# Expert tiles of 32 slots instead of 64: four column tiles, rows gathered for two experts at once, results scattered in 1 KB pieces

## The chip, the core and the metric

The kernel runs on one core of a Trainium2 chip. The time is that of one execution on the device in microseconds. Three runs of the kernel before took 806.93, 801.02 and 805.67 us; the median is 805.67.

## What is computed

One layer of a decoder for 256 prompt tokens and 8 sample tokens (T = 264) with 1024 features, all in fp32. The change touches the last part alone, the mixture of experts: each token chooses one of 4 groups and in it the best 2 of 8 experts, so 528 pairs of token and expert over 32 experts.

```
a = jnp.einsum('bld,edf->blef', h, w_gate)       # w_gate, w_up: 32 x 1024 x 256
u = jnp.einsum('bld,edf->blef', h, w_up)
act = jax.nn.silu(a) * u * combine[..., None]
return jnp.einsum('blef,efd->bld', act, w_down)  # w_down: 32 x 256 x 1024
```

Each expert's weights are 3 MB (1 MB each for gate, up and down). With the inputs of the reference an expert is chosen by 10 to 22 tokens, 16.5 in the mean; this follows from the reference's routing.

## The kernel before

Ahead of the experts stand the input projection, retention, block-sparse attention, output projections and the router. They read their weights through a ring of six 1 MB slots and end at about 510 us. Then VectorE works out the routing in a chain of small instructions and TensorE the positions of the tokens in each expert (L1093). A one-hot product, `row_table` (L1096 to L1101), writes for each expert and each of `CAP` = 64 slots the token that sits there. It is made twice, for output partitions 0 to 63 and 64 to 127. VectorE turns the first into `tidx_i` (L1505 to L1509, semaphore `t_idx`), the rows to gather, and the second into `sidx_i`, the rows to scatter to (L1510 to L1513). A slot without a token has an index out of bounds, and nothing is moved for it.

An expert then takes these steps. GpSimd gathers 64 rows of 4 KB into `xg` (L569 to L573). TensorE transposes them in eight pieces (`x_tr`, L1119) and VectorE copies them to `xgT` (`x_copy`). `gate_up` (L1129) holds the 64 rows as weights of a column tile of the array: two column tiles take the two halves of the 256 hidden columns of gate and up, 16 matmuls of 256 columns. An fp32 matmul is two instructions in the trace. ScalarE applies silu, VectorE multiplies (`hidden`), TensorE turns the result (`h_tr`, L1141), ScalarE copies it (`h_copy`), and `down` (L1147) makes the output in two column tiles, 4 matmuls of 512 columns. VectorE copies it out of PSUM (`y_copy`), and GpSimd scatters 128 pieces of 2 KB to `y_rows` (L574 to L577).

On TensorE the order for expert e is: gate and up of e, turned rows of e + 1, down of e - 1, turn of the hidden part of e (L1174 to L1179). Weights come through SyncE's queue into `SETS` = 5 sets of buffers; a set's gate and up are loaded again once `e_GU` says that they were used (L454 to L460), its down once `e_D` does. The first five sets are loaded during the stages before.

More tokens than slots would be served by overflow tiles: `XT = (2 * T) // (CAP + 1)` of them at most, 8. After expert 31 every engine goes through a loop of `XT` rounds (on SyncE and TensorE `XT // 2` rounds of two) and skips the bodies above the number of tiles that there are, none with these inputs (L596, L803, L1187, L1605). In the main stage VectorE also makes the tables for these tiles (`tile_counts`, `tile_tables`, `tile_experts`, `tile_rows`).

After the loop GpSimd waits for the scatters and signals `y_all` (L610 to L612). SyncE and ScalarE then read `y_rows` back, VectorE adds the two results of each token to the residual, and a last RMSNorm ends the kernel.

## Time and profile before

| | us |
|---|---|
| runs | 806.93, 801.02, 805.67 (median 805.67) |
| profiled execution, its time | 807.25 |
| its span, first to last instruction | 805.3 |
| TensorE matmuls busy | 694.6 (86%) |
| VectorE, ScalarE, GpSimd busy | 313.2, 129.4, 216.0 |
| mean granted TensorE clock | 0.947 |

HBM reads are 241.37 MB and writes 17.50 MB over the span. Busy TensorE counts matmuls whose ends are modelled and which overlap, so a high share does not say that it is the bound. The chain of work that ended last gives TensorE 49%, DMA 17%, VectorE 17%, the wait of SyncE's queue 7%, GpSimd 5%.

### The profile page before, as it was taken

How to read it: one execution, taken by the hardware profiler on the slowest of the kernel's cores; microseconds unless marked ns; L12 is line 12 of the kernel's file. 1: busy time of each engine (PE TensorE's matmuls, PEld its weight loads, DVE VectorE, ACT ScalarE, POOL GpSimd, SP SyncE). 2: the span in 40 equal slices, each digit the busy share in tenths (PEclk: the TensorE clock that was granted, in tenths of full speed). 3: DMA queues.
4: the chain of work that ended last, by engine and by line, in shares of the span. 5: the costliest groups of instructions: out<-in, count | busy, mean ns of one | idle time of the engine just before them, and what ended most of it. 6: DMA issues, size and time to landing. Idle time of an engine off the chain costs nothing.

```text
span 805.3 us, 11725 instructions
## 1 busy us (share of the span) xinstructions
PE 694.6 (86%) x3847; PEld 484.4 (60%) x3847; DVE 313.2 (39%) x1539; ACT 129.4 (16%) x381; POOL 216.0 (27%) x401
## 2 busy tenths in 40 slices
PE   3999996898999969999898999579999998888860
PEld 1888875687888756734434877355555554555530
DVE  2000895998768745600000221623432222112116
ACT  3122221232326222200010000300000000000001
POOL 0288992994000213200000000012222221221210
PEclk9999999899999989999999999769999999999995
DMA  9744899889977998579999794529999999999914
GB/s 314 197 147 139 287 332 386 300 290 332 340 270 246 340 373 278 176 292 406 400 409 364 232 420 189 210 85 382 394 398 395 398 381 388 402 398 399 357 70 161
DMA packets 98270, 247.21 MB, mean 307 GB/s; under 512 B 12156, under 2 KB 57852, under 8 KB 89890
## 3 DMA queue, kind: packets, MB, share of 16 engines
q1 hardware_dynamic: 83874, 220.28, 74.0%
q0 software_dynamic: 9456, 19.29, 7.2%
q10 hardware_dynamic: 4880, 6.88, 2.5%
q8 instruction: 32, 0.52, 0.3%
q14 instruction: 28, 0.23, 0.1%
HBM read 241.37 MB, written 17.50 MB: 321 GB/s over the span
## 4 chain that ended last, share of the span: by engine, by line
PE 49%; DMA 17%; DVE 17%; SPq 7%; POOL 5%; issue 3%; ACT 1%; POOLq 0%; DVEq 0%; ACTq 0%
PE zps L851 22%; DVE kall L1243 10%; PE nps L1136 10%; DMA ring_all<-in_w_up 6%; SPq L420 5%; DMA ring_all<-in_w_ret_o 4%; PE nps L1015 3%; PE zps L1126 2%; DMA kall<-in_cache_k 2%; PE bps L1156 2%; PE mps L1156 2%; DMA gain<-v_rows 2%; SPq L424 2%; PE zps L829 1%; DMA xs<-in_state_ret 1%
## 5 line engine op out<-in xcount | busy, mean ns | idle before, releaser
L851 PE MATMUL zps<-hT,ring_all 128*128 128x264 f32 x1152 | 279.1, 397 | 1.6 <-DVE hT L1424 1.0
L851 PEld LDWEIGHTS zps<-hT,ring_all 128*128 128x128 f32 x1152 | 220.6, 196 | 45.2 <-issue 3.7
L1243 DVE CUSTOM_DVE_ANT_0 kall<-kall,qb 128x128 f32<-128x128 f32 x512 | 141.1, 342 | 84.9 <-DMA kall<-in_cache_k 82.1
L570 POOL DMA_INDIRECT zatt<-h_rows,tidx_i x32 | 30.6, 956 | 217.6 <-DVEq L1509 200.1
L575 POOL DMA_INDIRECT y_rows<-zatt,sidx_i x32 | 32.5, 1015 | 172.4 <-DVE zatt L1582 172.4
L1015 PE MATMUL nps<-ring_all,zret 128*64 128x512 f32 x256 | 59.1, 600 | 5.4 <-DMA ring_all<-in_cache_v 4.3
L1136 PE MATMUL nps<-ring_all,retT 128*64 128x256 f32 x448 | 56.5, 409 | 8.0 <-DMA ring_all<-in_w_up 7.2
L1576 DVE TENSOR_TENSOR retT<-retT,nps 128x128 f32<-128x128 f32 x32 | 9.2, 288 | 127.6 <-ACT retT L790 85.7
L1136 PEld LDWEIGHTS nps<-ring_all,retT 128*64 128x64 f32 x448 | 35.9, 147 | 24.3 <-issue 9.3
L637 ACT ACTIVATE zt<-zps 128x264 f32<-128x264 f32 x48 | 18.6, 388 | 150.1 <-PE zps L851 150.1
L1411 DVE TENSOR_TENSOR hT<-zps,zatt 128x264 f32<-128x264 f32 x8 | 3.5, 433 | 96.5 <-PE zps L851 96.3
L1243 DVE DVE_READ_ACCUMULATOR2_ANT scores<- 128x1 f32 x512 | 40.7, 79 | 0.0
L1126 PEld LDWEIGHTS zps<-cst,zatt 64*128 64x128 f32 x256 | 30.6, 201 | 16.1 <-issue 16.1
L1015 PEld LDWEIGHTS nps<-ring_all,zret 128*64 128x64 f32 x256 | 16.7, 136 | 39.2 <-issue 25.2
L1126 PE MATMUL zps<-cst,zatt 64*128 64x64 f32 x256 | 34.9, 278 | 4.0 <-issue 4.0
L851 PE MATMUL zps<-retT,ring_all 128*128 128x264 f32 x128 | 29.7, 389 | 3.9 <-DMA ring_all<-in_w_ret_o 3.5
L790 ACT ACTIVATE retT<-nps 128x128 f32<-128x128 f32 x32 | 8.9, 278 | 145.1 <-PE nps L1136 131.7
L552 POOL DMA_DIRECT2D gain<-v_rows x16 | 8.8, 550 | 86.9 <-DVE xs L1326 82.5
L1570 DVE TENSOR_TENSOR retT<-zps,fT 128x512 f32<-128x512 f32 x32 | 22.1, 692 | 24.3 <-PE zps L1126 23.9
L851 PEld LDWEIGHTS zps<-retT,ring_all 128*128 128x128 f32 x128 | 23.9, 190 | 10.5 <-issue 6.0
L637 ACT ACTIVATE retT<-zps 128x128 f32<-128x128 f32 (+1 forms) x40 | 12.0, 300 | 110.7 <-PE zps L1145 91.8
L851 PE MATMUL zps<-attT,ring_all 128*128 128x264 f32 x128 | 28.7, 387 | 1.0 <-DVEq L1418 1.0
(326 smaller groups left out, 809.1 us busy)
## 6 DMA issues: line engine op xcount, KB each, us to landing
ring_all<-in_w_in SPq DMA_DIRECT2D x32, 1024.0 KB, 8.3
kall<-in_cache_k SPq DMA_DIRECT2D x64, 512.0 KB, 6.0
ring_all<-in_cache_v SPq DMA_DIRECT2D x64, 512.0 KB, 7.6
ring_all<-in_w_gate SPq DMA_DIRECT2D x14, 1024.0 KB
ring_all<-in_w_up SPq DMA_DIRECT2D x14, 1024.0 KB
ring_all<-in_w_down SPq DMA_DIRECT2D x14, 1024.0 KB
kall<-in_w_gate SPq DMA_DIRECT2D x6, 1024.0 KB
kall<-in_w_up SPq DMA_DIRECT2D x6, 1024.0 KB
```

The costliest lines, as they stand in the source:

```text
L420: sp.dma_start(gate_up_w[b][:, 2048 * a:2048 * (a + 1)], w[0, bass.ds(e, 1)].rearrange("o (p k) f -> p (o k f)", k=KT)).then_inc(gu_in[b], 16)
L424: sp.dma_start(down_w[b].rearrange("p (f n) -> p f n", f=FB), w_down[0, bass.ds(e, 1)].rearrange("o (f p) n -> p (o f) n", p=P)).then_inc( ...
L570: pool.indirect_dma_start(out=xg[par], out_offset=None, in_=h2_rows, in_offset=bass.IndirectOffsetOnAxis(ap=col, axis=0), bounds_check=T - ...
L575: pool.indirect_dma_start(out=y_rows.rearrange("r (c d) -> (r c) d", c=2), out_offset=bass.IndirectOffsetOnAxis(ap=col, axis=0), in_=ysb[p ...
L637: return act.activation(out, in_, ACT.Copy)
L851: mm = pe.matmul(zps[m % 2][:, 0:T], w[:, k, P * fb:P * (fb + 1)], rhs[:, k, :], start=(k == 0), stop=(k == KT - 1))
L1015: mm = pe.matmul(nps[0][64 * c:64 * (c + 1), :], pw[:, 512 * p + 64 * b:512 * p + 64 * (b + 1)], ring[n % RING][:, DM * k + 512 * c:DM * k ...
L1126: mm = pe.transpose(zps[par][:, CAP * k:CAP * (k + 1)], xg[par][:, k:DM:KT], ident[0:CAP, 0:CAP])
L1136: mm = pe.matmul(nps[par][CAP * c:CAP * (c + 1), 0:2 * P].rearrange("p (a f) -> p a f", a=2), xgT[par][:, CAP * k:CAP * (k + 1)], w[:, :, ...
L1156: mm = pe.matmul(y[CAP * c:CAP * (c + 1), 0:512], acT[par][:, CAP * f:CAP * (f + 1)], w[:, f, 512 * c:512 * (c + 1)], start=(f == 0), stop ...
L1243: ins = v.tensor_tensor_reduce(kh, kh, qb[b % 2][:, P * h:P * (h + 1)], 1.0, 0.0, ALU.mult, ALU.add, scores[:, pg, AH * b + h:AH * b + h + 1])
L1570: v.tensor_tensor(xgT[par].rearrange("p (k s) -> p k s", k=KT), zps[par][:, :].rearrange("p (k s) -> p k s", k=KT), fT[:, :].unsqueeze(2). ...
```

## The change

Tiles of 32 slots. Gate, up and down each go over four column tiles of 32; gate and up take 64 of the hidden columns per tile, down 256 output columns. Two experts' rows are gathered into one buffer of 64 partitions, transposed at once and copied at once. The row table is made for all 128 partitions before the first index is computed. The turn of the hidden part is two matmuls of 64 x 64 in a part of the gate-and-up bank instead of one transpose. The results are scattered as 128 pieces of 1 KB. `XT` becomes 528 // 33 = 16.

```diff
-CAP = 64
+CAP = 32
+TILES = P // CAP
+NPAIR = NE // 2
+EDGES = (T - 1) // CAP
 XT = (2 * T) // (CAP + 1)
...
-            def gather_for(e):
-                if e >= 2:
-                    pool.wait_ge(e_T, e - 1)
-                gather(e % 2, tidx_i[0:CAP, e:e + 1])
-
-            for e in range(3):
-                gather_for(e)
+            def gather_for(p):
+                if p >= 2:
+                    pool.wait_ge(e_T, p - 1)
+                gather(p % 2, xg[p % 2], tidx_i[0:2 * CAP, p:p + 1])
+
+            for p in range(2):
+                gather_for(p)
             pool.wait_ge(t_sidx, 1)
             for e in range(NE):
-                if e + 3 < NE:
-                    gather_for(e + 3)
+                if e % 2 == 0 and e // 2 + 2 < NPAIR:
+                    gather_for(e // 2 + 2)
                 pool.wait_ge(e_Dc, e + 1)
                 scatter(e % 2, sidx_i[:, e:e + 1])
...
             def row_table(out, a, b):
-                for c in range(2):
-                    for q in range(6):
-                        r = ROWS[q % 3]
-                        mm = pe.matmul(out[CAP * c:CAP * (c + 1), :], a[0:r, q, :], b[0:r, q, :], start=(q == 0), stop=(q == 5))
-                    mm.then_inc(t_tabs, 1)
+                for q in range(6):
+                    r = ROWS[q % 3]
+                    for c in range(TILES):
+                        mm = pe.matmul(out[CAP * c:CAP * (c + 1), :], a[0:r, q, :], b[0:r, q, :], start=(q == 0), stop=(q == 5),
+                                       tile_position=(0, CAP * c), skip_group_check=True)
+                mm.then_inc(t_tabs, 1)
...
-            def x_tr(par, x_value, h_used):
-
-                if h_used is not None:
-                    pe.wait_ge(e_Hc, h_used)
+            def x_tr(par, x_value, copied, rows):
+
+                if copied is not None:
+                    pe.wait_ge(e_Tc, copied)
...
                 for k in range(KT):
-                    for c in range(2):
-                        mm = pe.matmul(nps[par][CAP * c:CAP * (c + 1), 0:2 * P].rearrange("p (a f) -> p a f", a=2),
-                                       xgT[par][:, CAP * k:CAP * (k + 1)], w[:, :, k, P * c:P * (c + 1)],
-                                       start=(k == 0), stop=(k == KT - 1))
+                    for q in range(TILES):
+                        f = P * (q % 2) + 64 * (q // 2)
+                        mm = pe.matmul(nps[par][CAP * q:CAP * (q + 1), 0:P].rearrange("p (a f) -> p a f", a=2),
+                                       x[:, 2 * CAP * k:2 * CAP * k + CAP], w[:, :, k, f:f + 64], start=(k == 0), stop=(k == KT - 1),
+                                       tile_position=(0, CAP * q), skip_group_check=True)
...
-                pe.transpose(zps[par][:, 0:P], hid[par], ident).then_inc(e_H, 1)
+                for h in range(2):
+                    at = slice(64 * h, 64 * (h + 1))
+                    mm = pe.matmul(nps[par][at, 256:256 + 64], hid[par][at, :], ident[at, at], start=True, stop=True,
+                                   tile_position=(64 * h, 64 * h))
+                mm.then_inc(e_H, 1)
...
                 for f in range(FB):
-                    for c in range(2):
-                        mm = pe.matmul(y[CAP * c:CAP * (c + 1), 0:512], acT[par][:, CAP * f:CAP * (f + 1)],
-                                       w[:, f, 512 * c:512 * (c + 1)], start=(f == 0), stop=(f == FB - 1))
+                    for d in range(TILES):
+                        mm = pe.matmul(y[CAP * d:CAP * (d + 1), 0:256], acT[par][:, CAP * f:CAP * (f + 1)],
+                                       w[:, f, 256 * d:256 * (d + 1)], start=(f == 0), stop=(f == FB - 1),
+                                       tile_position=(0, CAP * d), skip_group_check=True)
...
-            for e in range(1, NE):
+            pair_x(0)
+            for e in range(NE):
                 expert_gate_up(e)
-                if e + 1 < NE:
-                    expert_x(e + 1)
-                expert_down(e - 1)
+                if e % 2 == 0 and e // 2 + 1 < NPAIR:
+                    pair_x(e // 2 + 1)
+                if e >= 1:
+                    expert_down(e - 1)
                 h_tr(e % 2, e + 1)
...
             v.wait_ge(t_tabs, 1)
-            d, w = rows_from(bps[0:CAP, 768:768 + NE], slice(0, CAP), 0, NE)
+            d, w = rows_from(bps[0:2 * CAP, 768:768 + NE], slice(0, 2 * CAP), 0, NE)
             link(v.tensor_scalar(w, d, T - 0.5, -float(T), ALU.is_gt, ALU.mult))
-            link(v.tensor_tensor(tidx_i[0:CAP, 0:NE], w, d, ALU.add))
+            for i in range(2):
+                at = slice(CAP * i, CAP * (i + 1))
+                ins = v.tensor_tensor(tidx_i[at, 0:NPAIR], w[at, i:NE:2], d[at, i:NE:2], ALU.add)
+            link(ins)
             v.sem_inc(t_idx, 1)
```

## Rows read from the trace of the kernel before

**Rows 1.** Stretches: start:end, length, PE, PEld, DVE, ACT, POOL busy, clock, DMA, GB/s.
```profile
520.00:540.00 20.00, 14.59 (x90) 11.17 (x90) 4.23 (x15) 1.78 (x3) 2.93 (x3) 0.59 0.09 20
544.00:548.00 4.00, 4.00 (x27) 2.05 (x25) 1.67 (x3) 0.56 (x2) 0.00 (x0) 1.00 0.97 328
600.00:650.00 50.00, 49.04 (x359) 27.40 (x355) 11.94 (x22) 4.16 (x15) 15.14 (x16) 1.00 1.02 394
700.00:750.00 50.00, 41.55 (x290) 25.71 (x286) 9.39 (x18) 3.33 (x12) 11.82 (x12) 0.97 1.02 399
760.00:775.40 15.40, 14.39 (x104) 8.38 (x104) 3.63 (x7) 1.18 (x5) 2.03 (x2) 1.00 0.42 164
```

**Rows 2.** Chain that ended last, one expert: start us, us, what.
```profile
653.18 0.26 PE zps L1145
653.45 3.60 PE nps L1136 x32
657.05 1.02 PE zps L1126 x8
658.07 1.87 PE bps L1156 x8
```

**Rows 3.** The same chain, from the last weights to the read back.
```profile
745.25 25.30 DMA ring_all<-in_w_up
...
770.68 3.67 PE nps L1136 x32
774.35 1.72 PE bps L1156 x8
...
776.70 1.96 PE mps L1156 x8
...
778.68 0.70 DVE zatt L1582
...
784.54 2.71 DMA ring_all<-y_rows
```

**Rows 4.** Branches of the empty loop, GpSimd and VectorE: ns, first and last start.
```profile
L596 POOLq COMPARE_BRANCH  x8: 40/45/53, 781.3 to 784.4; - x8
...
L1605 DVEq COMPARE_BRANCH  x8: 50/56/66, 780.1 to 783.8; - x8
```

**Rows 5.** Chain that ended last, start of the expert stage.
```profile
524.72 3.72 PE bps L1100 x24
...
531.08 1.13 PE zps L1126 x8
...
532.98 5.33 PE nps L1136 x32
```

**Rows 6.** TensorE in order of time, L923; the weight loads are of 267.15 to 267.25.
```profile
267.21 0.15 PEld L923 LDWEIGHTS mps<-xs,zatt 128*32 128x32 f32 x7 [0.33 <-issue]
...
267.21 0.64 PE L923 MATMUL mps<-xs,zatt 128*32 128x256 f32 x8
267.78 0.49 PE L851 MATMUL zps<-hT,ring_all 128*128 128x264 f32 x1
```

**Rows 7.** VectorE in order of time, first index.
```profile
526.65 0.18 DVE L1502 TENSOR_SCALAR zret<-bps 64x32 f32<-64x32 f32 x1 [2.04 <-PE bps L1100]
```

**Rows 8.** DMA of 529.8 to 530.8 (first gather) in 40 slices of 25 ns.
```profile
GB/s 0 0 0 0 1 2 329 329 328 328 0 0 0 0 0 328 0 164 0 0 164 164 0 328 1 0 0 0 0 1 0 0 0 0 0 0 0 0 0 0
```

**Rows 9.** DMA queues, 540 to 775 us: packets, MB, share of 16 engines.
```profile
q1 hardware_dynamic: 15096, 84.74, 91.9%
q0 software_dynamic: 4713, 3.98, 5.6%
```

**Rows 10.** The same of 40 to 66 us, projection weights in 1 KB pieces.
```profile
q1 hardware_dynamic: 4014, 4.05, 46.9%
```

**Rows 11.** An expert's gate and up after a wait, and the clock behind it.
```profile
720.30 5.36 PE L1136 MATMUL nps<-ring_all,retT 128*64 128x256 f32 x32 [1.85 <-DMA ring_all<-in_w_up]
...
720.80:724.00 3.20, 3.20 (x18) 2.29 (x16) 0.00 (x0) 0.00 (x0) 1.08 (x2) 0.50 1.00 410
```

**Rows 12.** TensorE in order of time, the overflow tiles' row table.
```profile
582.37 2.21 PE L1100 MATMUL bps<-zret 128*64 128x8 f32 x24
```

More of the change, by code:

```diff
@@ L50 @@
 _WIDTHS = [("ident", P), ("ones", P), ("upper", P), ("causal", 3 * P), ("rmask", RH * P), ("rdec", RH * P),
-           ("kdec", RH), ("rope", 3 * 4 * 64), ("edge", 4), ("slot", CAP), ("order", NE),
+           ("kdec", RH), ("rope", 3 * 4 * 64), ("edge", EDGES), ("slot", CAP), ("order", NE),
            ("val", 6), ("tile", XT), ("diag", NB * NB), ("own", AH),
-           ("before", 16), ("after", 16), ("spread", NB * AH), ("half", 1)]
+           ("before", 16), ("after", 16), ("spread", NB * AH), ("quarter", 1)]
 COL, _at = {}, 0
@@ L86, in shape_constants @@
     put("rope", rope.reshape(P, -1))
-    put("edge", np.tile(CAP * np.arange(1, 5) - 0.5, (P, 1)))
+    put("edge", np.tile(CAP * np.arange(1, EDGES + 1) - 0.5, (P, 1)))
     put("slot", np.tile(np.arange(CAP), (P, 1)))
@@ L97, in shape_constants @@
     put("spread", np.repeat(np.eye(NB), AH, 1), NB)
-    put("half", (i >= CAP)[:, None])
+    put("quarter", (i // CAP)[:, None])
     return c
@@ L245, in build @@
         rt = zr[:, 4096:6144]
-        xg = [zflat[0:CAP, DM * i:DM * (i + 1)] for i in range(2)]
-        ysb = [zflat[:, 2 * DM + 512 * i:2 * DM + 512 * (i + 1)] for i in range(2)]
+        xg = [zflat[0:2 * CAP, DM * i:DM * (i + 1)] for i in range(2)]
+        ysb = [zflat[:, 2 * DM + 256 * i:2 * DM + 256 * (i + 1)] for i in range(2)]
         gate_up_w = [None, None, kall[:, 0:4096], zdec_all[:, :], zr[:, 0:4096]]
@@ L567, in _, with gather @@
             pool.wait_ge(t_idx, 1)
-            def gather(par, col):
-                pool.indirect_dma_start(out=xg[par], out_offset=None, in_=h2_rows,
+            def gather(par, rows, col):
+                pool.indirect_dma_start(out=rows, out_offset=None, in_=h2_rows,
                                         in_offset=bass.IndirectOffsetOnAxis(ap=col, axis=0),
@@ L602, in _ @@
                     pool.sem_inc(pool_turn, 1)
-                    gather(0, tcol[0:CAP, 0:1])
+                    gather(0, xg[0][0:CAP, :], tcol[0:CAP, 0:1])
                     pool.wait_ge(e_Dc, j + (NE + 1))
@@ L795, in h_copy @@
                     act.wait_ge(e_D, used)
-                copy(acT[par], zps[par][:, 0:FB * CAP]).then_inc(e_Hc, 1)
+                copy(acT[par], nps[par][:, 256:256 + FB * CAP]).then_inc(e_Hc, 1)
             for e in range(NE):
@@ L1125, in x_tr, with gate_up @@
                 for k in range(KT):
-                    mm = pe.transpose(zps[par][:, CAP * k:CAP * (k + 1)], xg[par][:, k:DM:KT], ident[0:CAP, 0:CAP])
+                    mm = pe.transpose(zps[par][:, 2 * CAP * k:2 * CAP * k + rows], xg[par][0:rows, k:DM:KT], ident[0:rows, 0:rows])
                 mm.then_inc(e_T, 1)
-            def gate_up(par, b, n, landed):
-                pe.wait_ge(e_Tc, n)
+            def gate_up(par, x, b, x_copied, landed):
+                pe.wait_ge(e_Tc, x_copied)
                 pe.wait_ge(gu_in[b], landed)
@@ L1560, in tile_rows @@
             def tile_rows():
-                v.wait_ge(t_tabs, 4)
+                v.wait_ge(t_tabs, 2)
                 d, w = rows_from(bps[:, 768:768 + XT], slice(0, P), NE, NT)
@@ L1564, in tile_rows, with x_copy @@
                 link(v.tensor_tensor(tidx_i[:, NE:NT], w, d, ALU.add))
-                link(v.tensor_scalar(sidx_i[:, NE:NT], d, 2.0, cc("half"), ALU.mult, ALU.add))
+                link(v.tensor_scalar(sidx_i[:, NE:NT], d, float(TILES), cc("quarter"), ALU.mult, ALU.add))
                 v.sem_inc(t_sidx, 1)
-            def x_copy(par, n):
+            def x_copy(par, n, rows):
                 v.wait_ge(e_T, n)
-                v.tensor_tensor(xgT[par].rearrange("p (k s) -> p k s", k=KT), zps[par][:, :].rearrange("p (k s) -> p k s", k=KT),
-                                fT[:, :].unsqueeze(2).to_broadcast([P, KT, CAP]), ALU.mult).then_inc(e_Tc, 1)
+                v.tensor_tensor(xgT[par].rearrange("p (k s) -> p k s", k=KT)[:, :, 0:rows],
+                                zps[par][:, :].rearrange("p (k s) -> p k s", k=KT)[:, :, 0:rows],
+                                fT[:, :].unsqueeze(2).to_broadcast([P, KT, rows]), ALU.mult).then_inc(e_Tc, 1)
             def hidden(par, n):
                 v.wait_ge(e_sg, n)
-                v.tensor_tensor(hid[par], hid[par], nps[par][:, P:2 * P], ALU.mult).then_inc(e_ac, 1)
+                v.tensor_tensor(hid[par], hid[par], nps[par][:, 64:128], ALU.mult).then_inc(e_ac, 1)
             def y_copy(par, n, out_value):
@@ L1593, in _ @@
                     hidden(e % 2, e + 3)
-                if e + 3 < NE:
-                    x_copy((e + 3) % 2, e + 4)
+                if e % 2 == 0 and e // 2 + 2 < NPAIR:
+                    x_copy(e // 2 % 2, e // 2 + 3, 2 * CAP)
                 if e == 0:
@@ L1606, in _ @@
                 with v.If(extra > j):
-                    x_copy(0, j + (NE + 1))
+                    x_copy(0, j + (NPAIR + 1), CAP)
                     hidden(0, j + (NE + 1))
```

42 lines of the change are left out of this document (18 added, 24 removed).

## Prediction

> **What bounds the kernel now.** I read the stages first. Up to the routing the change touches nothing. Between 520 and 540 us the DMA engines stand at a share of 0.09: all five buffer sets are full and the expert stage has not begun. From then on they stand at 1.02, moving 394 and then 399 GB/s [rows 1]. The expert weights are 32 times 3 MB; at that rate one expert is 3.146 MB / 0.397 = 7.9 us.
>
> Next the chain inside the stage. An expert costs TensorE 0.26 + 3.60 + 1.02 + 1.87 = 6.75 us (turned hidden, gate and up, turned rows, down) [rows 2]. That is less than 7.9, so TensorE eats the lead of the five sets and then waits: the chain ends in the landing of the last `w_up`, issued at 745.25, landed at 770.54 [rows 3]. Behind it stand 8.84 us to the end of the last copy at 779.38, and then a thing easily missed: GpSimd goes through the loop over overflow tiles at L596, empty for these inputs, in 8 rounds, and only then are the results read back, at 784.54 [rows 3, 4]. So three places can move the end: when the first set is freed (532.98 + 5.33 = 538.31 [rows 5]), how fast the weights stream, and what follows the last landing.
>
> **The parts.** TensorE's steady work falls: gate and up from 3.60 to about 1.8, down from 1.87 to 0.94, the turned rows from 1.02 an expert to 1.02 a pair. All of that between the first and the last expert is worth nothing: the weights' 7.9 us cover it, as they already cover 6.75.
>
> *Do four tiles overlap?* The only four-tile matmuls of before are those at L923: eight of 256 columns, 0.64 us, the next group starting 0.57 us after them [rows 6]. Two column tiles do 32 of the same length in 3.60, 0.113 each [rows 2]; 0.57 / 8 is 0.071, and that holds one change of shape and the fill. Half the columns per instruction at twice the number, spread on twice the tiles, gives half of 3.60. I take 1.8. The far end is no gain at all. The turn of the hidden part is one instruction of 0.26 on the whole array now and becomes two small matmuls, some 0.3.
> Against it speaks a rule of the Trainium skill (TensorE: Matmul & The Clock Gate, section "Wait — 56ns, not 53.3ns?"): with decoding in microcode each matmul takes some 62 ns of issue, which would bound short matmuls. By it the 64 of gate and up would take 4.0 us. The trace does not agree: seven weight loads of L923, each with a matmul behind it in the program, have begun within 0.04 us [rows 6].
>
> *Waits.* The transposes of a pair now wait for the copy of the pair two before, 15 us old in the stream; GpSimd's gather waits for those transposes, and behind it on its queue stands the scatter of an expert that TensorE has not finished by then. Neither is late, since a gather is issued two pairs ahead. Cover: the same 7.9 us.
>
> *Start, on the path.* (a) The row table: now 24 instructions in 3.72 us at half clock [rows 5], the index computed once the first 12 are done (VectorE starts at 526.65 [rows 7], 1.93 after 524.72). Then 48, the four tiles taking turns, before the index may start. As 12 steps of four they take what 12 take now: 0; one after another 48 × 0.155 = 7.4, or +5.5. By rows 6 I take 0. One more short VectorE instruction, +0.2 as its neighbours [rows 7]. (b) The first gather brings two experts' rows. Its data now move within about 0.5 us of an idle machine [rows 8]; twice the valid rows, +0.5. The transposes of 64 slots are the same eight instructions. (c) The first gate and up takes 5.33 at half clock and then full [rows 5]; half of the columns' time at half clock is 3.5: -1.8 (ends 0 and -2.7). So the first set is freed 1.1 us sooner. (d) The second is freed at 544.3 today and the queue runs thin: 328 GB/s in 544 to 548 [rows 1] against 394 is a loss of 0.67 us. Then it comes well ahead: -0.6. Start: -1.7, from -3.5 to +5.5.
>
> *Stream.* Weights are unchanged: 84.74 MB, 91.9% of the engines' time; gathers and scatters take 5.6% [rows 9]. Results go out in 1 KB pieces. In the projection stage, where pieces are 1 KB, 4.05 MB took 46.9% of 26 us on 16 engines [rows 10], 20.8 GB/s each; the expert weights have 84.74 MB / (0.919 × 235 × 16) = 24.5. For the 2.2 MB of results that is 0.8 us at most; the gathers halve in number. I take +0.2, ends 0 and +1.
>
> *Tail, on the path.* From the last `w_up`: 3.67 gate and up, 1.72 down, 0.3 turn, 0.3 copy, 1.96 down, 0.70 copy [rows 3]. At full clock 1.8 + 0.95 + 0.3 + 0.3 + 1.0 + 0.4 and 0.7 of gaps = 5.4; but `w_down` of the last expert comes after `w_up`, and DMA engines are still at work until 775.4 [rows 1], 4.9 after it, which makes it 6.4. That would be -2.4. But TensorE will then have waited some 4 us before each expert. Once today it waited 1.85 us and the granted clock was half behind it: 5.36 instead of 3.67 [rows 11]. At half clock the tail is 3.6 + 1.9 + 0.6 + 0.3 + 1.9 + 0.4 plus gaps, about 8.8, the time of now. Halfway: -1.3, ends 0 and -2.4. In the stream half clock is harmless: 2 × 3.4 = 6.9 us an expert, still under 7.9.
>
> *The empty loop.* The diff does not name it: `XT` is 2T // (CAP + 1), 8 at 64 slots and 16 at 32. Its branches come once a round; on GpSimd the eight at L596 stand from 781.3 to 784.4, 3.1 / 7 = 0.44 us a round [rows 4]. It runs after the last scatter is issued, and the read back at 784.54 follows it directly. Eight rounds more: +3.5. The scatter's own landing is shorter and stays hidden. VectorE has the same loop at 0.53 a round [rows 4], +4.2, but is not wanted until the read back has landed at 787.25 [rows 3], now 3.3 us after its loop; that shrinks to 2.6. The Trainium skill (Advanced Engine Details and Errata, section "Control Flow Timing") gives a compare-and-branch about 108 ns; with two a round that would be 1.7 us for the eight. The row says twice that, and the row decides.
> At VectorE the tables of overflow tiles also double (16 rounds at L1554 instead of 8); it is busy 11.94 of 50 us there [rows 1], and the DMA backlog covers it. Without that cover it would be about 3 us.
>
> Sum: -1.7 + 0.2 - 1.3 + 3.5 = **+0.7 us**. The profiled execution took 807.25 (span 805.3), 1.6 over the median of 805.67; against its own time it comes to 807.9, against the median to **806.4**.
>
> **The rivals.**
> *Even finish.* Between 760 and 775.4 the DMA share is 0.42 [rows 1]: the sixteen engines do not end together, the last weights wait for a few of them. That is 6.5 us of full work; evenly spread all would be done at 766.5 and `w_up` at 763.9, 6.6 sooner. If the unevenness comes from gathers and scatters, whose valid rows are the first slots of each tile, four pieces on other partitions might spread it. Against it: no row shows which engine takes which piece, and a pair's slots start at 0 and 32 just as aligned as 0 and 64 did. Result 799.8, and with the favourable ends (1.8 more at the start, 1.1 in the tail) 796.9. Chance 0.12.
> *The tiles do not overlap* (slower). The place is TensorE in the stream: an expert has 64 + 16 matmul instructions instead of 32 + 8. At 1.1 us for the rest it becomes the bound from (7.9 - 1.1) / 80 = 0.085 us each. Serial in one tile, the table's 24 short ones took 2.21 us, 0.092 each [rows 12], so the point is near: at 0.1 us an expert costs 9.1, and 27 experts 32 us more, 838. For it: weight loads double in number too. Against it rows 6. Chance 0.08.
> *The loop is hidden or the start gains everything*: for instance if the scatter's landing or something else decides the read back; then -3 us, 802 to 803. The chain shows loop and read back touching [rows 3, 4]. Chance 0.15.
> *Start or table goes wrong* but TensorE keeps up: serial tables +5.5, no gain at the first expert; 810 to 813. Chance 0.10.
>
> **The numbers.** My forecast, about 806, has 0.55. One measurement of before reached from 801.02 to 806.93, so 1% (8 us) is about what can be told from no change. Range: from 800.5, which takes in the ends of start and tail and the lower runs, to 812, the table's serial end; the slow rival and the best of the even finish lie outside. Faster by over 1% (under 797.6) only where the even finish comes with the good ends, 0.09; slower (over 813.7) the second rival and a little of the last, 0.10; within 1%, 0.81.
>
> **What would show it.** Gate and up at about 1.8 us at full clock and nearer 3.6 where the granted clock is half; the first set's refill issued about 537.2 instead of 538.35; the stream still at a share near 1.0 and waits of TensorE on `w_up` in nearly every expert; sixteen rounds instead of eight in GpSimd's loop, and 8.7 us, not 5.2, from the last copy to the read back. Wrong would be: a stream that ends more than 3 us sooner than the start explains, a TensorE without waits, or a read back that does not wait for the loop.

## The result, and the profile after

The changed kernel takes 800.51 us in the median of 20 runs, the kernel before 805.73 in 20 runs beside it: ratio 0.9943, interval 0.9921 to 0.9964, so 4.6 us faster. The ratio is that of the fast runs alone, while the medians are of all runs, two slow ones of the changed kernel included, of which one took 974.96 us. The forecast was 806.4, in effect no change. Two further measurements of the same kernel gave 0.9934 and 0.9939. The profiled execution took 801.3 us, with a span of 799.3 (before 807.25 and 805.3) and a mean granted clock of 0.888 instead of 0.947.

The stretches of the changed kernel, columns as in [rows 1]:

```profile
520.00:540.00 20.00, 12.57 (x236) 10.63 (x239) 5.21 (x21) 1.67 (x4) 2.92 (x3) 0.62 0.24 77
544.00:548.00 4.00, 3.25 (x88) 2.50 (x86) 2.93 (x18) 0.45 (x2) 0.00 (x0) 1.00 1.00 408
600.00:650.00 50.00, 34.04 (x640) 24.19 (x640) 7.65 (x20) 3.12 (x14) 10.88 (x11) 0.76 1.02 393
700.00:750.00 50.00, 29.80 (x512) 24.72 (x508) 5.73 (x14) 2.45 (x11) 7.95 (x8) 0.73 1.02 399
760.00:775.40 15.40, 6.64 (x112) 4.19 (x104) 1.50 (x4) 0.67 (x3) 2.95 (x3) 0.72 0.20 77
```

TensorE's busy time has fallen by some 30% and its clock with it, the DMA share stands at 1.02 as before. The stage is still bound by the weights, which shows in the waits: from 652.94 us on TensorE waits for `w_up` before every gate and up, 14 times in all. The chain that ended last, start of the stage:

```profile
523.51 1.38 PE bps L1103 x46
...
526.67 3.81 DMA zatt<-h_rows,tidx_i
...
530.57 1.13 PE zps L1130 x8
...
532.47 3.22 PE nps L1141 x64
```

The table of 48 instructions takes 1.38 us where 24 took 3.72, and the first gate and up 3.22 instead of 5.33 [rows 5]. From SyncE's queue the first refill, and from TensorE in order of time the last two experts:

```profile
535.76 0.34 SPq L423 DMA_DIRECT2D ring_all<-in_w_gate  x1
```

```profile
755.22 3.64 PE L1141 MATMUL nps<-ring_all,retT 128*32 128x128 f32 x64 [3.53 <-DMA ring_all<-in_w_up]
...
762.91 2.84 PE L1141 MATMUL nps<-ring_all,retT 128*32 128x128 f32 x64 [2.10 <-DMA ring_all<-in_w_up]
...
768.20 1.07 PE L1165 MATMUL mps<-ring_all,retT 128*32 128x256 f32 x16 [0.54 <-DMA ring_all<-in_w_down]
```

TensorE waits 2 to 4 us for `w_up` here and then works at half clock, 3.64, or partly so. The last down waits for its own weights. Then the chain's last copy, and the empty loop on GpSimd, sixteen rounds at 0.44, after which the results are read back at 778.36; its eight rounds are in [rows 4]:

```profile
769.33 0.43 DVE zatt L1593
...
778.36 0.33 SPq L478
...
779.15 7.71 DMA ring_all<-y_rows
```

```profile
L599 POOLq COMPARE_BRANCH  x16: 40/45/53, 771.6 to 778.2; - x16
```

The two profiled spans side by side. I call the time from the first refill's issue to the start of the last gate and up **the stream**: before 770.68 - 538.35 = 232.3 us.

| part | before | after | difference | forecast |
|---|---|---|---|---|
| up to the row table | 524.72 | 523.51 | -1.2 | not the change |
| table to first refill | 13.63 | 12.25 | -1.4 | -1.1 |
| the stream | 232.33 | 227.15 | **-5.2** | -0.6 + 0.2 |
| last gate and up to the end of the last copy | 8.70 | 6.85 | -1.9 | -1.3 |
| last copy to read back | 5.16 | 8.60 | +3.4 | +3.5 |
| read back to the end | 20.76 | 20.94 | +0.2 | 0 |

Sum -6.0. One row is off by 4.8 us, nearly all of the error: the stream.

### The profile page after: what moved, and what is told of

Read it like the earlier page. It is cut to its first block, busy times and chain, and to the rows that moved or that the text cites. A ratio compares the mean times of both kernels' runs of the same rounds, so it can differ in the third digit from the quotient of the medians.

```text
span 799.3 us, 14422 instructions
## 1 busy us (share of the span) xinstructions
PE 619.6 (78%) x5143; PEld 468.0 (59%) x5143; DVE 294.8 (37%) x1548; ACT 125.7 (16%) x381; POOL 200.1 (25%) x385
## 3 DMA queue, kind: packets, MB, share of 16 engines
q0 software_dynamic: 7152, 19.28, 7.1%
## 4 chain that ended last, share of the span: by engine, by line
PE 41%; DMA 27%; DVE 16%; issue 7%; POOL 5%; SPq 3%; ACT 0%; POOLq 0%; DVEq 0%; ACTq 0%
PE zps L854 21%; DVE kall L1251 9%; DMA zdec<-in_w_up 6%; PE nps L1141 6%; DMA gain<-v_rows 4%; DMA ring_all<-in_w_ret_o 4%; PE nps L1018 3%; DMA zret<-in_w_up 3%; DMA kall<-in_cache_k 3%; DMA ring_all<-in_w_down 3%; PE mps L1165 2%; SPq L423 2%; PE zps L832 1%; PE zps L1130 1%; PE bps L1165 1%
## 5 line engine op out<-in xcount | busy, mean ns | idle before, releaser
L1251 DVE CUSTOM_DVE_ANT_0 kall<-kall,qb 128x128 f32<-128x128 f32 x512 | 139.4, 338 | 85.2 <-DMA kall<-in_cache_k 82.6
L573 POOL DMA_INDIRECT zatt<-h_rows,tidx_i x16 | 15.6, 972 | 207.2 <-DVEq L1520 199.3
L1587 DVE TENSOR_TENSOR retT<-retT,nps 128x64 f32<-128x64 f32 x32 | 7.1, 221 | 130.2 <-ACT retT L793 130.2
L1141 PE MATMUL nps<-ring_all,retT 128*32 128x128 f32 x896 | 39.4, 349 | 20.1 <-DMA ring_all<-in_w_up 19.4
L1130 PE MATMUL zps<-cst,zatt 64*128 64x64 f32 x128 | 17.6, 298 | 40.6 <-issue 35.4
L1141 PEld LDWEIGHTS nps<-ring_all,retT 128*32 128x32 f32 x896 | 34.5, 143 | 22.2 <-issue 20.0
L1130 PEld LDWEIGHTS zps<-cst,zatt 64*128 64x128 f32 x128 | 15.3, 200 | 44.9 <-issue 44.9
L793 ACT ACTIVATE retT<-nps 128x64 f32<-128x64 f32 x32 | 7.1, 223 | 142.4 <-PE nps L1141 142.4
L1580 DVE TENSOR_TENSOR retT<-zps,fT 128x512 f32<-128x512 f32 x16 | 11.1, 692 | 48.2 <-PE zps L1130 48.2
L832 PE MATMUL nps<-cst,zt 128*128 128x128 f32 x144 | 24.0, 276 | 5.2 <-ACT zt L640 5.2
```

The lines of the kernel that those rows point to most:

```text
L573: pool.indirect_dma_start(out=rows, out_offset=None, in_=h2_rows, in_offset=bass.IndirectOffsetOnAxis(ap=col, axis=0), bounds_check=T - 1, ...
L832: return pe.transpose(out, in_, ident[0:rows, 0:rows])
L1130: mm = pe.transpose(zps[par][:, 2 * CAP * k:2 * CAP * k + rows], xg[par][0:rows, k:DM:KT], ident[0:rows, 0:rows])
L1141: mm = pe.matmul(nps[par][CAP * q:CAP * (q + 1), 0:P].rearrange("p (a f) -> p a f", a=2), x[:, 2 * CAP * k:2 * CAP * k + CAP], w[:, :, k, ...
L1251: ins = v.tensor_tensor_reduce(kh, kh, qb[b % 2][:, P * h:P * (h + 1)], 1.0, 0.0, ALU.mult, ALU.add, scores[:, pg, AH * b + h:AH * b + h + 1])
L1580: v.tensor_tensor(xgT[par].rearrange("p (k s) -> p k s", k=KT)[:, :, 0:rows], zps[par][:, :].rearrange("p (k s) -> p k s", k=KT)[:, :, 0:r ...
```

## The experiments

Each was timed beside the kernel before. "Stream" is from each kernel's own two rows, as above, and "end" is the mean DMA share in the last 20 us of the stream, up to the start of the last gate and up. Both are from one profile each.

| kernel | ratio to before, interval | stream, us | end |
|---|---|---|---|
| before | 1 | 232.3 | 0.72 |
| changed | 0.9943 [0.9921, 0.9964] | 227.2 | 0.83 |
| changed, second and third measurement | 0.9934 [0.9903, 0.9965], 0.9939 [0.9909, 0.9969] | 228.0, 228.3 | 0.82, 0.81 |
| changed, loops of 8 rounds | 0.989 [0.9837, 0.9943] | 227.2 | 0.84 |
| changed, matmuls twice | 1.0319 [1.0262, 1.0376] | bound by TensorE |  |
| changed, slots spread | 0.9876 [0.9833, 0.9919] | 221.3 | 0.99 |
| changed, one gather per expert | 0.9912 [0.9878, 0.9945] | 227.5 | 0.83 |
| changed, late refills | 0.9921 [0.9891, 0.9951] | 229.2 | 0.84 |
| changed, 128 empty rows more per expert | 0.9962 [0.9933, 0.9991] | 229.9 | 0.81 |
| changed, 2 KB pieces, 64 of them | 0.9961 [0.9931, 0.9992] | 229.4 | 0.73 |
| changed, 2 KB pieces, 128, valid at 0 and 32 | 1.0084 [1.0052, 1.0116], 1.0063 [1.003, 1.0095] | 238.0, 237.6 | 0.58, 0.59 |
| changed, 2 KB pieces, 128, valid at 0 and 64 | 0.997 [0.9942, 0.9999] | 230.4 | 0.78 |
| before, slots spread | 0.9879 [0.9847, 0.9912] | 226.4 | 1.00 |
| before, loops of 16 rounds | 1.0029 [0.9996, 1.0061] | 233.1 | 0.69 |
| before, gathers of 32 slots | 0.9988 [0.9955, 1.0021] | 234.3 | 0.70 |
| before, spread, loops skipped | 0.9871 [0.9827, 0.9914] | 223.3 | 1.00 |
| changed, spread, loops skipped | 0.9785 [0.9747, 0.9822] | 221.5 | 0.99 |
| the same with 64 pieces of 2 KB | **0.9752** [0.971, 0.9794] | 220.8 | 1.00 |

### The changed kernel again

> The changed kernel as it is, on the same chip as the next three, as their base. Its profile against the first one shows how much the length of the weight stream varies by itself. Theory pace (the weight stream is shorter because the first sets come free sooner): again about 4.6 us under the kernel before, 227 to 229 us from the first refill's issue to the landing of the last w_up. Theory traffic (gathers and scatters cost the DMA engines less): the same. Theory chance (the profiled pair happened to differ): the stream is as likely 230 as 227.

> The changed kernel unaltered, beside the two kernels with 2 KB pieces on the same chip: ratio 0.993 to 0.995, a stream of about 227 us.

The gain repeats, and so does a stream of 227 to 228 us. The kernels of before that leave the order of the slots and the scatter alone have 232.3, 233.1 and 234.3.

### The empty loop

Five loops over 8 rounds instead of 16 in the changed kernel; `XT` = 16 in the one before.

```diff
-            with pool.Fori(0, XT) as j:
+            with pool.Fori(0, ROUNDS) as j:   # ROUNDS = 8, all five engines
```

```diff
-XT = (2 * T) // (CAP + 1)
+XT = 16
```

> The changed kernel with 8 rounds of the loop over overflow tiles instead of 16 (it leaves out serving the ninth and later overflow tiles, which these inputs don't have). If the loop stands on the path, 16 rounds cost 3.5 us: this is 3.5 us faster than the changed kernel, and 5.2 us pass between last copy and read back instead of 8.6. If the loop is hidden behind the scatter's landing: no difference.

> The kernel before with XT set to 16, so that the empty loop and the overflow tables have the size of the changed kernel, and nothing else. Loop on the path: 3.5 us slower than the kernel before, 8.7 us from last copy to read back. Its profile is also a second look at the stream of the kernel before: theory chance has 227 to 231 us from first refill to last w_up, theories pace and traffic 231 to 232.

From the last copy to the read back eight rounds take 5.1 us in the changed kernel (its copy ends at 768.5, below), and sixteen take 8.7 in the one before. Of the time, the first gains 0.44% (3.5 us, with overlapping intervals), the second loses 0.29% (2.3 us). Sign and size fit the forecast step; the interval of the second just includes zero.

```profile
768.12 0.42 DVE L1594 COPY zatt<-mps 128x256 f32<-128x256 f32 x1 [2.10 <-PE mps L1166]
```

```profile
773.61 1.22 SPq L479 DMA_DIRECT2D ring_all<-y_rows  x3
```

### How much TensorE has to spare

```diff
-                for k in range(KT):
+                for k in [*range(KT), *range(KT)]:
...
-                for f in range(FB):
+                for f in [*range(FB), *range(FB)]:
```

> The changed kernel with the matmuls of gate and up and of down done twice (the same result), so that an expert costs TensorE about 6.5 us at full clock, as in the kernel before (6.75), with the DMA traffic unchanged. Theory pace: the refills come as late as before, the stream is about 5 us longer, and with 2 to 4 us more in the tail (less, since the clock stays up) the time is 6 to 9 us over the changed kernel. Theory traffic: the stream keeps its length after the first refill, only start (about 3 us at half clock) and tail cost, 3 to 5 us in all.

Ratio 1.0319, 30 us more than the changed kernel. The theories had 6 to 9 and 3 to 5 us, so this run doesn't decide between them; it shows that doubled, TensorE is the bound. Between 560 and 760 us SyncE's queue waits 122 us for gates and ups to be used, in the changed kernel 23. The DMA share is near 1 here as well:

```profile
600.00:650.00 50.00, 41.77 (x932) 31.75 (x936) 6.39 (x18) 2.47 (x11) 8.86 (x9) 0.93 0.99 383
```

So a share near 1 does not by itself say that the weights bound a stage; which engine waits for which has to be read with it. An expert costs about 8 us though its matmuls sum to 6.5 or so. In the chain of the doubled kernel it stops in the middle of gate and up and waits for nothing that the profile shows:

```profile
640.75 1.97 PE nps L1141 x62
642.71 2.00 issue
644.71 0.31 PE nps L1141 x3
...
648.24 3.19 PE nps L1141 x86
651.43 0.82 issue
652.25 1.50 PE nps L1141 x42
```

Instruction packets on DMA are 64 in this kernel; the changed one has 42, the one before 32:

```profile
q8 instruction: 64, 1.05, 0.5%
```

That the gaps are TensorE waiting for its own instructions behind a full DMA is argued from this count, not isolated.

### The order of the slots

The same edit in both kernels: the partitions of a tile hold the slots 0, 16, 1, 17, ... (0, 32, 1, 33, ... in the kernel before) instead of 0, 1, 2, ..., so that successive tokens of an expert go to every other partition.

```diff
-    put("slot", np.tile(np.arange(CAP), (P, 1)))
+    at = np.arange(CAP)
+    put("slot", np.tile(at // 2 + CAP // 2 * (at % 2), (P, 1)))
```

> The changed kernel with another order of slots: slot s of a tile sits at partition 2s (s under 16) or 2(s - 16) + 1, so that the 10 to 22 used slots lie over all 32 partitions and not in the first ones. If the DMA engines end unevenly because the rows of gathers and scatters fall on a few of them, all 16 end together: the last w_up lands up to 6 us sooner, the share stays near 1 until then, and the kernel is 5 to 8 us faster than the changed one. If the unevenness has another source: no difference, or up to 1 us slower from more small packets.

> The kernel before with its 64 slots laid alternately (slot s at partition 2s, slot 32 + s at partition 2s + 1), nothing else. If rows in the first slots load a few DMA engines, it gains what the changed kernel gained by the same, 5 to 7 us. If TensorE's pace (6.75 us an expert at full clock against 7.7 of the shorter stream) were near the bound, less.

The mechanism of the even finish is real: 0.6% (4.7 us) in the changed kernel and 1.2% (9.7 us) in the one before. The stream is 6 to 7 us shorter in the changed kernel. In the one before it is 6 us shorter in this profile and 9 in the second kernel with spread slots (223.3, below). The last 20 us of the stream in the kernel before, the changed one and the changed one spread, in this order:

```profile
750.68:770.68 20.00, 17.18 (x108) 9.49 (x104) 4.54 (x8) 1.39 (x5) 2.99 (x3) 0.91 0.72 280
```

```profile
742.91:762.91 20.00, 12.59 (x201) 9.71 (x197) 2.63 (x7) 1.34 (x6) 2.90 (x3) 0.73 0.83 338
```

```profile
730.31:750.31 20.00, 10.40 (x201) 7.44 (x198) 2.63 (x7) 1.34 (x6) 2.96 (x3) 0.91 0.99 402
```

Spread, the share stays near 1 to the end. The same number of valid rows moves, only their places differ. The change itself already makes the end more even: in three profiles of before the share is 0.69 to 0.72, in seven of changed kernels with slots in order and 1 KB pieces 0.81 to 0.84. Against 1.02 throughout, 0.72 and 0.83 over 20 us leave 6.0 and 3.8 us of full work undone. By this estimate the more even end is 2.2 of the 5.2 us by which the change shortens the stream.

### Refills and gathers

Late refills hold SyncE's queue back once, at the second and third set, as TensorE's slower start did before:

```diff
+                    if e == 5:
+                        sp.wait_ge(e_GU, 3)
+                    if e == 6:
+                        sp.wait_ge(e_D, 3)
...
+                if e == 5:
+                    sp.wait_ge(e_D, 2)
+                if e == 6:
+                    sp.wait_ge(e_GU, 5)
```

> The changed kernel with the second, third and fourth refill (and the downs between them) held back by added waits, so that they are issued about 6, 12 and 15 us after the first one, as in the kernel before (6.0, 12.8, 19.5), instead of 3, 6 and 11. Everything else as changed. Theory pace: the stream is 3 to 5 us longer and the time 3 to 5 us over the changed kernel. My own term for it in the prediction: 0.6 us. Theory traffic: under 1 us.

The second to fourth refill came 6.3, 11.4 and 15.3 us after the first, the fifth at 16.8, where the kernel before has 26.8. The stream is 229.2, 0.9 to 2.0 longer than in the three measurements of the changed kernel: neither theory's size, and not much more than these three differ among themselves (1.1). The total (0.9921) doesn't show it, so what refills are worth rests on one profile.

```diff
-                gather(p % 2, xg[p % 2], tidx_i[0:2 * CAP, p:p + 1])
+                for i in range(2):
+                    gather(p % 2, xg[p % 2][CAP * i:CAP * (i + 1), :], tidx_i[0:CAP, 2 * p + i:2 * p + i + 1])
```

> The changed kernel with a gather of 32 slots for each expert instead of one of 64 for a pair (transposes and copies still for the pair). The valid rows moved are the same, the gather instructions and their completion writes double. Theory traffic, if the pairing is what relieved the DMA engines: the stream from first refill to last w_up goes from 227 back towards 231 us and the time up 3 to 4 us. Theory pace: no difference within 1 us, for the refills of the first sets come as early (or 0.5 us sooner, as the first gather is shorter).

Gathering for two experts at once brings nothing (0.9912, stream 227.5).

The kernel before, gathering only the first 32 of its 64 slots, and the changed kernel with one more gather per expert of 128 rows that are all out of bounds:

```diff
-                gather(e % 2, tidx_i[0:CAP, e:e + 1])
+                gather(e % 2, tidx_i[0:32, e:e + 1])
```

```diff
+                pool.indirect_dma_start(out=nobody[:, :], out_offset=None, in_=h2_rows.rearrange("r (c d) -> (r c) d", c=16),
+                                        in_offset=bass.IndirectOffsetOnAxis(ap=none_i[:, 0:1], axis=0),
+                                        bounds_check=16 * T - 1, oob_is_err=False).then_inc(pad_in, 16)
```

> The kernel before with gathers of the first 32 of the 64 slots (the other 32 are never used with these inputs; the tile's lower rows keep what they held, and nothing of them is scattered). 32 empty descriptors fewer an expert. Theory traffic: 1 to 3 us faster than the kernel before, stream 229 to 231 instead of 231.6 and 232.5. Else within 0.5 us.

> The changed kernel with one more gather an expert, of 128 indices that are all out of bounds, into a tile that nobody reads: it moves no row, but adds 32 times 128 empty descriptors and 16 completion writes to the DMA engines. The change itself took away about 2,300 packets under 512 B. Theory traffic, if empty descriptors are what slowed the stream: 4 to 7 us slower than the changed kernel, stream 231 to 234. Otherwise: under 1.5 us, as 4600 packets of about 11 ns over 16 engines are 3.2 us of DMA time at the very most and GpSimd's microsecond for it is idle time.

With 128 empty rows more an expert the ratio is 0.2 to 0.3% higher, with overlapping intervals, and the stream 1.6 to 2.8 us longer; leaving out 32 of them gives nothing that can be measured. The change has 62 + 15.5 empty indices an expert instead of 95 + 47.5, 65 fewer, so about 1 us by the first run, an estimate. Counted in packets it looks different: GpSimd's queue has 9456 in the kernel before, 7152 in the changed one and 8176 with the empty rows. At 2 us for 1024 packets the 2304 that the change saves would be worth 4.5 us. Against it stands the kernel before with gathers of 32 slots: 8432 packets, 1024 fewer, and no gain. Whether the number of small packets matters is not settled by these runs.

### The scatter

Results in 2 KB pieces as before, all else the change. With `PIECES` = 64 the pieces come from partitions 0 to 63; with `PIECES` = 128 the upper 64 are always out of bounds.

```diff
-        ysb = [zflat[:, 2 * DM + 256 * i:2 * DM + 256 * (i + 1)] for i in range(2)]
+        ysb = [zflat[0:PIECES, 2 * DM + 512 * i:2 * DM + 512 * (i + 1)] for i in range(2)]
...
-                    for d in range(TILES):
-                        mm = pe.matmul(y[CAP * d:CAP * (d + 1), 0:256], acT[par][:, CAP * f:CAP * (f + 1)],
-                                       w[:, f, 256 * d:256 * (d + 1)], start=(f == 0), stop=(f == FB - 1),
+                    for d in range(2):
+                        mm = pe.matmul(y[CAP * d:CAP * (d + 1), 0:512], acT[par][:, CAP * f:CAP * (f + 1)],
+                                       w[:, f, 512 * d:512 * (d + 1)], start=(f == 0), stop=(f == FB - 1),
```

> The changed kernel with its results in 2 KB pieces: down goes over two column tiles of 32 partitions and 512 columns, as wide as before, and 64 pieces an expert are scattered from partitions 0 to 63, some 33 of them valid. Everything else is the change. TensorE's down is about 1.9 us instead of 0.9, hidden but for the last one. Theory A (the 1 KB pieces on all four quarters spread the writes over the DMA engines, and that is the gain of the stream left open): the stream is 2 to 3 us longer than the changed kernel's, with the last down +0.9: ratio 0.997 to 0.999. Theory B (the number of empty pieces is what costs): 31 empty instead of 62, the stream is 0.5 to 1.5 us shorter, ratio 0.992 to 0.994 with the longer last down. Rival C (neither): stream as in the changed kernel, ratio 0.994 to 0.996.

> As the kernel with 2 KB pieces from 64 partitions, but 128 pieces an expert, of which the upper 64 are always out of bounds: about 33 valid and 95 empty, as many of each as in the kernel before. Theory B (empty pieces cost, by the run with 128 empty rows an expert 2 to 3 us for 128): 1.0 to 1.5 us longer than with 64 pieces. Theory A and rival C: no difference from the kernel with 64 pieces within its interval.

64 pieces: 0.9961, stream 229.4, 1.1 to 2.2 over the changed kernel, between what theory A and rival C had. 128 pieces: 1.0084, ten microseconds more. None of my theories had that. 64 empty pieces should have cost 1 us. So I held the number fixed and moved the valid ones: 33 valid and 95 empty in both kernels, in one from partitions 0 and 32 on, in the other from 0 and 64 on as in the kernel before.

```diff
-    put("quarter", np.where(i < 2 * CAP, i // CAP, 4 * T)[:, None])
+    put("quarter", np.where(i % 64 < CAP, i // 64, 4 * T)[:, None])
...
-                        mm = pe.matmul(y[CAP * d:CAP * (d + 1), 0:512], acT[par][:, CAP * f:CAP * (f + 1)],
+                        mm = pe.matmul(y[64 * d:64 * d + CAP, 0:512], acT[par][:, CAP * f:CAP * (f + 1)],
```

> As the kernel with 2 KB pieces from 128 partitions (ratio 1.0084), with one difference: down's second column tile is the third of the array, so that the valid pieces lie at partitions 0 and 64 on, as in the kernel before, instead of 0 and 32 on. 33 valid and 95 empty pieces in both. Theory A (where the valid pieces lie among the 128 decides how evenly the DMA engines are loaded, not how many are empty): some 5 to 6 us shorter, the stream near the 232 us of the kernel before, ratio 1.000 to 1.004. Theory B (the number of empty pieces decides): no difference, 1.006 to 1.011.

> The kernel with 2 KB pieces from 128 partitions, valid ones at 0 and 32 on, unaltered, on the same chip as the one with the pieces apart: ratio 1.006 to 1.011, a stream of about 237 us.

0.997 against 1.0063 on the same chip: 7.5 us for the places alone, with 8176 packets on GpSimd's queue in both. It is more than theory A had (5 to 6), and at 0 and 64 the stream of 230.4 is shorter than the 232 it had. The end of the stream with the valid pieces at 0 and 32, and with them at 0 and 64:

```profile
752.98:772.98 20.00, 13.62 (x170) 7.68 (x170) 3.19 (x7) 1.12 (x5) 1.97 (x2) 0.82 0.59 232
```

```profile
746.58:766.58 20.00, 14.59 (x243) 8.32 (x241) 4.24 (x9) 1.80 (x8) 2.98 (x3) 0.91 0.78 297
```

That is 8.6 and 4.8 us of full work undone, 3.8 of the 7.2 by which the streams differ. The stretches of the first kernel with the valid pieces at 0 and 32:

```profile
540.00:740.00 200.00, 136.09 (x2056) 74.72 (x2052) 42.61 (x131) 11.21 (x50) 37.64 (x38) 0.82 1.01 388
...
700.00:750.00 50.00, 36.18 (x492) 20.41 (x492) 8.20 (x16) 2.69 (x12) 8.92 (x9) 0.77 1.00 369
```

and with them at 0 and 64:

```profile
540.00:740.00 200.00, 142.85 (x2084) 79.61 (x2078) 42.81 (x132) 11.43 (x51) 36.72 (x37) 0.82 1.02 395
...
700.00:750.00 50.00, 35.58 (x548) 20.37 (x548) 7.72 (x16) 2.91 (x13) 9.90 (x10) 0.83 1.02 394
```

Read the last two columns: at nearly the same busy share the engines move 388 instead of 395 GB/s, and 369 instead of 394 near the end. So it is not only that some engines end later: while all are busy, fewer bytes move too.

One more thing sets the kernels with 2 KB pieces apart. Between 545 and 740 us TensorE waits for a gather at nearly every pair (inferred as in the last section) and hardly ever for `w_up`: 12 waits of 47.3 us in all at 0 and 32 (second measurement), 12 of 47.9 us at 0 and 64. In the changed kernel it waits for gathers 8 times, 35.4 us, and then for the weights. Their `down` takes 1.9 us instead of 1.07 at full clock, and it stands between a gather and the scatter after which the next one is issued. So what the places do is shown between these two kernels. Against the changed kernel each of them also has the longer `down`, and 1024 packets more.

Over the same 200 us as above the kernel before, the changed one and the changed one spread have 393, 398 and 402, in this order:

```profile
540.00:740.00 200.00, 185.59 (x1331) 109.12 (x1333) 52.55 (x130) 14.71 (x53) 52.22 (x53) 0.98 1.02 393
```

```profile
540.00:740.00 200.00, 124.70 (x2352) 95.54 (x2356) 37.51 (x134) 11.82 (x53) 39.70 (x40) 0.78 1.02 398
```

```profile
540.00:740.00 200.00, 128.41 (x2351) 94.23 (x2344) 35.51 (x119) 11.83 (x53) 39.78 (x41) 0.84 1.02 402
```

### The best version

The spread slots and, around each of the five loops, one branch that skips it when there is no overflow tile; in the kernel before, in the changed one, and in the changed one with 64 pieces of 2 KB.

```diff
-            with pool.Fori(0, XT) as j:
-                with pool.If(extra > j):
+            with pool.If(extra > 0):
+                with pool.Fori(0, XT) as j:
+                    with pool.If(extra > j):
```

> The kernel before with spread slots and the tested loop: what these two are worth without the change. 7 to 9 us (spread) and 1.9 to 3.3 (8 rounds of 0.44, the rest bounded by the scatter's landing): ratio 0.983 to 0.987, so 3 to 6 us behind the changed kernel with the same two.

> The changed kernel with the spread slots, and on every engine the loop over overflow tiles inside one test for whether there are any. It should add both gains: 5.3 us of the spread slots and 16 rounds less on GpSimd, 7.1 us; from last copy to read back about 3.3 us, then bounded by the scatter's landing. 12 us under the changed kernel, ratio to the kernel before 0.977 to 0.981.

> The best version so far (used slots spread, empty loops skipped as a whole, 0.9785) with its results in 2 KB pieces from 64 partitions. If the number of pieces matters once they are spread: 0.975 to 0.977; if only evenness counts: 0.978 to 0.981, the last down being 0.9 us longer.

The changed kernel reaches 0.9785 (17.3 us under before), as expected, and 0.9752 with 2 KB pieces (20 us); these two can't be told apart, so the question put in the last expectation stays open. In the first, the read back follows the last copy after 3.1 us instead of 8.6:

```profile
758.32 0.42 DVE L1598 COPY zatt<-mps 128x256 f32<-128x256 f32 x1 [1.35 <-PE mps L1169]
```

```profile
761.87 1.20 SPq L480 DMA_DIRECT2D ring_all<-y_rows  x3
```

The kernel before has 0.9871 with the same two edits, 0.1% less than with spread slots alone (0.9879), where skipping its loop should have given 1.9 us or more; the intervals are too wide to tell. The changed kernel with both edits is 0.9% ahead, 6.9 us where 3 to 6 was expected: the change no longer pays for eight rounds.

## Why the prediction was wrong, step by step

- **The bound.** Right: the weights, before and after. But TensorE waits for `w_up` in 14 of 32 experts, not in "nearly every" one; up to 656 us it waits for gathers.
- **Four tiles overlap.** Right. At full clock 64 instructions of gate and up take 1.89 to 1.96 us (forecast 1.8), down 0.86 in the chain (0.94). With a weight load behind each, that is 0.03 us an instruction. The Trainium skill (TensorE: Matmul & The Clock Gate, section "Wait — 56ns, not 53.3ns?") has 62 ns a matmul where decoding is done in microcode: by it they would take 4.0. The trace does not agree, as foreseen; no run shows which decoding is in force.
- **Waits.** "Neither is late" was wrong, without a price. TensorE does wait for gathers in the changed kernel, as shown below; the named cover, the weights' 7.9 us, holds.
- **Start.** -1.4 where -1.1 stood. Table at no cost: it got cheaper, VectorE starting 1.41 after the table's first matmul instead of 1.93. From the first gather's issue to the transposes it is 3.90 us instead of 2.82, +1.1 (+0.5). The first gate and up gained 2.1 (1.8). Right in sum.
- **The stream: the step that failed.** It said -0.6 for the refills and +0.2 for 1 KB pieces, "ends 0 and +1"; the profiles show -5.2, and the repeats of both kernels 4.0 us at the least. That is the sign of being wrong that the prediction had named, a stream that ends over 3 us sooner than the start explains. The term that failed is the scatter: I priced the pieces by their size (bytes per second of 1 KB packets elsewhere), which left no room for a gain. By its own figures it is 1.0 us at most too, not 0.8. The runs show that the places of the valid pieces among the 128 count, up to 7.5 us. With a scatter like that of before put back (2 KB, valid at 0 and 64 of 128) the stream is 230.4, 2.1 to 3.2 longer than the changed kernel's. Not all of this need be the scatter's, since that kernel has a longer `down` and more packets, and their ratios (0.997 and 0.9934 to 0.9943) have overlapping intervals. Refills that come in time were put at 0.6, read from 544 to 548 us alone; by one profile they are worth 1 to 2. Added to 230.4 that makes 231.4 to 232.4, where before has 232.3 to 234.3. So the two can account for the gap or most of it, but each rests on single profiles, and how the gap is divided stays open. Fewer gather rows and the pairing have no measurable share.
- **Even finish.** Given 0.12, with the words that no row shows which engine takes which piece. The mechanism exists and the change brings a part of it: the share at the end of the stream rises from 0.72 to 0.83, some 2.2 us, where spread slots bring 0.99 and shorten the stream by 6 to 9 us. That the time came near that rival's 799.8 is in part luck: it counted 6.6 us for an even end, of which 2.2 came, and the rest came from elsewhere in the stream, from start and tail. It was wrong to end this at an argument from alignment, where the same row left an uneven end worth 6.6 us unexplained; for the scatter, 0 and 32 are not as good as 0 and 64.
- **Tail.** -1.9 where -1.3 stood: right in kind. The last gate and up was at half clock for a part (2.84), and the last `w_down` set the end.
- **Empty loop.** +3.4 where +3.5 stood, shown in the profiles by both edits of the number of rounds, while neither time is clear of the noise by itself.
- **Slower rivals.** A serial table and serial tiles are excluded. Doubled, TensorE does become the bound, at 128 + 32 instructions an expert: the point from which that rival decides lies between.
- **The sign.** With -1.5 from the refills and -2.6 from the scatter instead of -0.6 and +0.2, the same sum gives -3.0 against the measured -4.6; these two are my estimates from the runs above. The median of 800.51 stands at the lowest edge of the range (800.5), which was made of other terms. The profile has 0.3 more at the start, 0.6 more in the tail and 1.1 more in the stream than these terms.

What stays open is how a position in the list of indices is mapped to a DMA engine; no view shows single engines, so the law by which 0 and 32 are bad and 0 and 64 are better isn't known. A map in which positions 32 apart share engines and positions 64 apart do not would fit these two kernels; it is not shown.

## What to carry to other kernels

Where a stage is bound by streaming weights, ask of every small transfer beside them not only how many bytes it has but where its valid rows lie among its descriptors: at a DMA share of 1.0 the GB/s of the same stretch shows a loss, the share at the end of the stream shows unevenness, and a permutation of the slots is a cheap test. Compare ends by the time since the stream began or before its last landing, not at the same microsecond of two profiles. Look for loop counts that a new tile size changes silently, and skip an empty loop with one branch. Faster matmuls off the path bring little but lower clock: here a good part of the gain came with the edit of the scatter, which was only a by-product.

## What the runs showed of the hardware that was not expected

- The place of valid pieces in an indirect DMA of 128 is worth 7.5 us in a 230 us stream (0.997 against 1.0063), at equal counts of valid and empty pieces.
- Empty indices are cheap: 128 an expert, 4096 in all, made the stream 1.6 to 2.8 us longer in one profile, together with the 32 gathers that carry them; the times alone don't show it.
- A gather beside saturated queues takes long: in the changed kernel eight in a row, issued from 549.48 to 648.35, are followed 7.3 to 8.4 us later by their transposes, before which TensorE stood idle for 0.9 to 7.4 us. The first one, on the idle machine at 526.67, landed after 3.81. GpSimd issues a pair's gather only behind a scatter, which waits for the copy of an expert's output, so it is not two pairs ahead in time but one and a half experts. In the changed kernel, two gathers on GpSimd and the transposes of the two pairs that they bring on TensorE, in order of time:

```profile
634.40 0.97 POOL L573 DMA_INDIRECT zatt<-h_rows,tidx_i  x1 [0.30 <-issue]
...
648.35 0.97 POOL L573 DMA_INDIRECT zatt<-h_rows,tidx_i  x1 [0.30 <-issue]
```

```profile
642.81 1.11 PE L1130 MATMUL zps<-cst,zatt 64*128 64x64 f32 x8 [4.75 <-issue]
...
655.76 1.07 PE L1130 MATMUL zps<-cst,zatt 64*128 64x64 f32 x8 [0.87 <-issue]
```

From issue to transposes it is 8.41 and 7.41 us, beside a median of 7.6 from issue to landing for the gathers of 640 to 700 us. The profile names no releaser ("issue"); that it is the landing is inferred from these times.
- A TensorE that waits before each expert has a lower clock: 0.73 to 0.76 granted in the two stretches above where before has 1.00 and 0.97, and a gate and up takes 3.64 us (1.2 GHz) instead of 1.89 (2.4 GHz) behind a wait. Off the path it costs nothing; in the tail it can cost up to 1.8 us, an estimate from these two durations.
- A round of an empty loop with a condition costs 0.44 us on GpSimd, twice in agreement: sixteen rounds from 771.6 to 778.2. The Trainium skill (Advanced Engine Details and Errata, section "Control Flow Timing") has some 108 ns for a compare-and-branch, 0.22 for the two of a round. The round takes twice that, while each of its two branches takes only 45 to 50 ns in the trace; the rest is other register instructions and the gaps between.
